# Unused products ahead of the second sums of squares and of the next layer's first chunk, at three layer crossings

## The reference, cut to what matters

```
y_l, y_c = mixer(h_l, h_c, need_ctx=need_ctx)          # ends with a product: (...) @ w_out
x_lat = x_lat + gt_l * rmsnorm(y_l, g_post)            # first root of a mean of squares
x_ctx = x_ctx + gt_c * rmsnorm(y_c, g_post)
# next layer
h_l = rmsnorm(x_lat, g_pre) * (1.0 + sc_l) + sh_l      # second root of a mean of squares
h_c = rmsnorm(x_ctx, g_pre) * (1.0 + sc_c) + sh_c
...  = h @ w_in
```

## Time and profile before

| | |
|---|---|
| median of 3 runs | 2997.91 us |
| profiled execution | 2989.49 us, span 2987.6 us |
| TensorE products (PE) busy | 2793.4 us, 93% of the span |
| TensorE weight loads (PEld) busy | 2298.3 us, 77% |
| VectorE (DVE) busy | 1565.3 us, 52% |
| ScalarE (ACT) busy | 1223.8 us, 41% |
| GpSimd (POOL) busy | 886.4 us, 30% |
| granted TensorE clock, mean | 0.977 |

### The profile page before, as it was taken

How to read it: one execution, slowest core, us unless ns; L and a number is a source line. 1 busy time by engine, 2 the same in 40 slices (tenths; PEclk the granted TensorE clock), 3 DMA queues, 4 the chain that set the end, 5 groups by cost and what they waited for, 6 DMA issues and landing times.

```text
span 2987.6 us, 39329 instructions
## 1 busy us (share of the span) xinstructions
PE 2793.4 (93%) x15720; PEld 2298.3 (77%) x15720; DVE 1565.3 (52%) x3126; ACT 1223.8 (41%) x2112; POOL 886.4 (30%) x636
## 2 busy tenths in 40 slices
PE   6989989999999999999999979999899999989997
PEld 4766878777877788878977768777798878878785
DVE  6677290162842876760268471254537238562583
ACT  4335234553213222242268354544443236443582
POOL 4611564403553444433200123200323320124301
PEclk8999999999999999999999989999999999999998
DMA  8303452301333555541300121100211230123101
GB/s 319 134 29 120 183 211 85 113 1 71 114 113 116 216 191 190 217 155 57 106 16 2 57 86 70 57 1 21 107 57 66 97 141 13 66 85 131 46 2 71
DMA packets 54293, 293.73 MB, mean 98 GB/s; under 512 B 4512, under 2 KB 8928, under 8 KB 24288
## 3 DMA queue, kind: packets, MB, share of 16 engines
q1 hardware_dynamic: 22464, 163.59, 15.5%
q10 hardware_dynamic: 31648, 127.63, 11.3%
HBM read 268.10 MB, written 17.86 MB: 96 GB/s over the span
## 4 chain that ended last, share of the span: by engine, by line
PE 56%; DVE 11%; ACT 3%; issue 2%; PEldq 0%; DMA 0%; DVEq 0%; PEld 0%; ACTq 0%
PE psum L467 14%; PE psum L469 14%; PE psum L468 14%; PE psum L1919 2%; PE psum L3551 2%; PE psum L1759 2%; PE psum L1782 2%; PE psum L1940 2%; DVE pair_row L1973 1%; PE psum L1929 1%; DVE y L2617 1%; PE psum L1763 1%; PE psum L1771 1%; DVE pair_prob L1982 1%; ACT L1004 1%
## 5 line engine op out<-in xcount | busy, mean ns | idle before, releaser
L454 POOL TENSOR_TENSOR w_lo<-raw,w_hi 128x512 fp32r<-128x512 f32 x612 | 859.9, 1437 | 2042.8 <-ACT w_hi L462 2042.8
L467 PE MATMUL psum<-a_hi,w_hi 128*128 128x512 f32 (+1 forms) x1848 | 697.5, 377 | 48.5 <-DVE a_lo L1162 17.0
L468 PE MATMUL psum<-a_lo,w_hi 128*128 128x512 f32 (+1 forms) x1848 | 686.4, 371 | 0.0
L469 PE MATMUL psum<-a_hi,w_lo 128*128 128x512 f32 (+1 forms) x1848 | 685.9, 371 | 0.0
L467 PEld LDWEIGHTS psum<-a_hi,w_hi 128*128 128x128 f32 x1848 | 350.9, 190 | 120.8 <-issue 23.5
L468 PEld LDWEIGHTS psum<-a_lo,w_hi 128*128 128x128 f32 x1848 | 350.8, 190 | 63.5 <-issue 3.4
L469 PEld LDWEIGHTS psum<-a_hi,w_lo 128*128 128x128 f32 x1848 | 350.2, 189 | 61.5
L462 ACT ACTIVATE w_hi<-raw 128x2048 fp32r<-128x2048 f32 x153 | 292.5, 1912 | 241.0 <-DMA raw<-stream 209.0
L467 PE MATMUL psum<-w_hi,a_hi 128*128 128x256 f32 (+1 forms) x608 | 199.0, 327 | 5.2 <-DVE a_lo L2654 4.4
L905 DVE SCALAR_TENSOR_TENSOR ada_temp<-ada_ring,psum 128x1024 f32<-128x1024 f32 x160 | 185.7, 1217 | 28.4 <-ACT psum L1134 14.1
L468 PE MATMUL psum<-w_lo,a_hi 128*128 128x256 f32 (+1 forms) x608 | 194.1, 319 | 0.0
(11 more groups left out here) (431 smaller groups left out, 4723.1 us busy)
## 6 DMA issues: line engine op xcount, KB each, us to landing
raw<-stream SPq DMA_DIRECT2D x153, 1024.0 KB, 4.9
ada_ring<-ada ACTq DMA_DIRECT2D x72, 1024.0 KB, 6.2
x_in<-xres ACTq DMA_DIRECT2D x3, 3072.0 KB, 12.5
xres<-x_in ACTq DMA_DIRECT2D x3, 2048.0 KB, 8.4
partner<-gq ACTq DMA_DIRECT2D x4, 1024.0 KB, 9.5
xres<-x_in ACTq DMA_DIRECT2D x1, 3072.0 KB, 9.5
own_raw<-stream SPq DMA_DIRECT2D x3, 1024.0 KB, 5.1
xres<-x_in ACTq DMA_DIRECT2D x3, 1024.0 KB, 4.8
```

The costliest lines, as they stand in the source:

```text
L454: last = pool.tensor_tensor(k.lo_of(s)[:, cols], k.raw_of(s)[:, cols], k.hi_of(s)[:, cols].bitcast(F32), ALU.subtract)
L467: pe.matmul(out, lhs[0], rhs[0], start=start, stop=False)
L468: pe.matmul(out, lhs[0], rhs[1], start=False, stop=False)
L469: return pe.matmul(out, lhs[1], rhs[0], start=False, stop=stop)
```

## The change

Two kinds of edit. In `sum_up`, for the second sum only, TensorE now waits for four chunks' squares and then issues 24 unused products, ahead of the wait for `gathered`; as `sum_up` is shared, this is issued six times (three latent, three context). And `dense` gets `fill=10` in Bin, Cv and A3q, ahead of the first two tiles.

```
@@ sum_up @@
         if turn == 0:
             pe.wait_ge(*self.total_in)
         else:
+            pe.wait_ge(self.squared.sem, self.squared.at(4))
+            self.k.keep_busy(pe, self.k.psum[:, 7, :], 24)
             pe.wait_ge(self.gathered.sem, self.gathered.at(KC - 1))
         pe.matmul(self.k.psum[:, 7, 0:self.t1 - self.t0], self.k.cst("ones"), self.total[:, self.t0:self.t1],
                   start=True, stop=True).then_inc(self.summed.sem, 1)
@@ gqa_layer, section A3q @@
-          act_tile=into(q, ACT.Copy, parts, -A_SCALE), barrier=False, lead=2, fill=5 if both else 0,
+          act_tile=into(q, ACT.Copy, parts, -A_SCALE), barrier=False, lead=2, fill=5 if both else 10,
@@ mla_layer, section Bin @@
-    dense(k, block, ["Bin"], None, act_tile=take_raw, barrier=False, lead=2, n_banks=7, side=context,
+    dense(k, block, ["Bin"], None, act_tile=take_raw, barrier=False, lead=2, n_banks=7, fill=10, side=context,
@@ mlstm_layer, section Cv @@
-    dense(k, block, ["Cv"], None, barrier=False, lead=2, n_banks=7, side=context, act_tile=take_value,
+    dense(k, block, ["Cv"], None, barrier=False, lead=2, n_banks=7, fill=10, side=context, act_tile=take_value,
```

## The result

| | before | after |
|---|---|---|
| median, 5 runs each | 2997.91 us (2995.33 to 3000.24) | 3012.37 us (3010.43 to 3014.53) |
| ratio, 95% interval | | 1.0048 (1.0033 to 1.0062) |
| profiled execution | 2989.49 us, span 2987.6 | 3010.43 us, span 3008.6 |
| granted clock, mean | 0.977 | 0.986 |

The change makes the kernel slower, by 14.5 us in this measurement and by 17.5 us in the means of a second one (e5_again). Predicted was 3021, with 3011 to 3031 as range. The median lies in the range, but only 1.4 us above its lower end; the differences, +14.5 and +17.5, lie under the +20 to +28 that had 76%, and the first of them in the +8 to +15 of rival 3. The two profiled executions lie 20.9 us apart.

The account below looks back on a forecast made before the run. TensorE, busy 93% of the span, was taken to bound the kernel. Delays at six places summed to +23.1 us, giving 3012.6 on the profiled 2989.49 and, with the runs' median 8.4 us above it, 3021; range 3011 to 3031.

Parts of the forecast that it names:

- rival 3: Cost partly absorbed, by a hidden last context crossing or shorter VectorE steps: +8 to +15 us, 3006 to 3013; chance 10%.
- What an unused product costs: Each product leaves two records of 0.215 us: 24 products cost 10.3 us of TensorE, 10 cost 4.3 us.
- rival 1: Products are cheap, 24 in 2.6 us, and mostly fit into idle time: -8.5 us, 2989; chance 4%.
- The new wait binds nowhere: At all second sums TensorE arrives after the fourth square is done, so the 24 products begin on arrival.
- D: Context tokens, layer 1 to 2: only 2.71 us idle before, root 7.0 us late, tile 8 follows: +7.0 us.
- A: Latent tokens, layer 0 to 1: root 3.6 us late, warm leading group 10.9 us instead of 13.4: +1.5 us.
- Place by place: Delays at the six latent and context crossings: 1.5, 1.2, 3.6, 7.0, 1.5 and 8.3, together +23.1 us.
- Nothing behind takes it back: Behind the last context sum, from 2695 to 2760, TensorE waits only for that sum, so the delay stays.
- C: Latent tokens, layer 1 to 2: sum 3.6 us later, clock gives back nothing beyond the sum: +3.6 us.
- E: Latent tokens, layer 2 to 3: same course as the latent crossing of layer 0 to 1, +1.5 us.
- the bounds on GpSimd: GpSimd's weight work stretches VectorE's steps; falling otherwise beside shifted steps, it may move each crossing 1 to 2 us either way.
- F: Context tokens, layer 2 to 3: products run to 2703.3 instead of a sum at 2695.01, all TensorE's time: +8.3 us.

Follow-up runs that it names:

- e5_again: The changed kernel once more, unaltered, beside many runs of the kernel before on the same chip: ratio 1.0060, mean difference +17.5 us.
- e11: The change with 12 unused products instead of 24 at all six places, fill of 10 kept: ratio 1.0015 to the kernel before, +3.8 us.
- e8: Kernel before plus only the blocks of 24 in the three context crossings, no latent blocks, no fill: ratio 1.0059, mean difference +17.2 us.
- e2: The change without fill=10, the six blocks of 24 left: ratio 1.0090 to the kernel before, mean difference +28.5 us.
- e1: The kernel before, unchanged, profiled a second time: ratio 0.9994, profiled execution 2991.98 us.
- e4: The change without the context blocks: 24 products ahead of the latent second sums, fill of 10 kept; ratio 1.0013 to the kernel before, +5.1 us.

## Why the prediction was right, and where its size was off

- **What an unused product costs** (10.3 us for 24): right. The blocks take 10.36 us from their start to the sum, e11 gives 0.43 us a product a second time. The short price, rival 1, is refuted. (Two small slips in the prediction change nothing: four times 109 ns for 24 products is 10.5 us, not 10.3, and the upper bound of the places is 25.2, not 25.3.)
- **The new wait binds nowhere**: right. No row of a block has a bracket in the profile after, so they begin where TensorE arrives (e8, sum 3 to 4: D grows by 7.5 us, which is 10.3 less an idle time of 2.7).
- **The clock.** That blocks and fill keep it up: right (1.00 throughout). That the gain is the warm leading group and the warm sum: right, e2 shows that the fill is needed for it. Its size in A goes by one profile: the leading group lasts 11.1 us instead of 13.4 there, and 12.6 in the second profile of the kernel before (e1), where the clock came up earlier.
- **Place by place**: right to 0.2 us between the two profiled executions, 23.0 against 23.1. Some of this closeness is luck: with e1 in place of the profile before, A is +2.2 and D +7.4, and the sum +24.0.
- **"Nothing behind takes it back"**: right. From the last marks of the third crossing to the end the distance between the two profiles only shrinks from 21.7 to 21.0, that of the spans.
- **The step whose size was off** is the one from the profile to the runs: "The median of the runs lies 8.4 us above this execution; the same 23.1 on it gives 3021". It takes whatever makes other executions longer as something that the change leaves alone. Behind it stands the reading "the sum begins there instead of 1738.82": I took the idle time of 5.47 us ahead of the latent sums, three times nearly equal, for a constant of the kernel. It has two values, 5.5 and 8.7, and in the profiled execution all three crossings had the small one. In a crossing that goes the long way the block of 24 covers 3.26 us more. For C this is measured once: 48.77 us from sum 1 to 3 with the block, 48.32 in e8's second crossing without, so +0.45 instead of +3.6. For A and E it is an estimate, 1.4 less 3.26 = -1.9, as no profile has these two the long way without products.
- How far this explains the runs: the places, +23.0 on the all-short 2989.49, give 3012.5 for the changed kernel, and its mean was 3012.2 both times. So the differences of 14.3 and 17.5 follow from how far the kernel before lay above 2989.49, 8.4 and 5.2 us. At 3.26 us a crossing these would be 2.6 and 1.6 crossings of three the long way; the eleven of 24 counted in the profiles would be 1.4. That the whole offset is this and nothing else isn't shown. All-short executions differ too (2989.49, 2991.98 in e1, and single runs of the kernel before go down to 2984.4), three crossings of 3.26 can make 9.8 us of a spread of 14, and by the same sum e4 should be 2995.8 (mean 2997.0) and e2 3016.4 (mean 3020.4). Why the share of the long way should differ from chip to chip stays open.
- The sentence in the bounds on GpSimd ("each crossing may move by 1 to 2 either way") had the cause in view and half its size, but as a shift that could go either way. The profile was all on the short side, so against it other executions of the kernel before can only be longer. Rival 3 named a smaller difference too, but not for this reason: F wasn't hidden (+8.35).

## What to carry to other kernels

On this kernel, unused products that keep the clock up are paid in full (0.43 us each) from the moment at which the wait that they fill would have ended: count them against the idle time of each place, and don't share one count between places with 8.4, 2.7 and 1.8 us. A helper that is called from several places (here both kinds of crossing) carries an edit to all of them. And an idle time read from one execution is one draw: profile the same kernel more than once and look at the spread of its runs before fitting anything to tenths of a microsecond. Two profiles wouldn't have been enough here: before and e1 are both the short way in all three crossings.

## What was not expected of the hardware

GpSimd and VectorE, both on 512-column f32 tensor operations with two inputs, slow each other when they overlap: VectorE's pair of 1.29 us takes 3.48, and GpSimd's first operation takes 3.47 where VectorE's pair goes ahead of it, 1.7 where it doesn't. With GpSimd's start 0.42 us ahead of VectorE's either can win, with nothing between (25.2 or 28.45 us for the stretch), and the outcome changes from one execution of the same program to the next, by a step of 3.26 us. Most other distances repeat to about 0.02 us; those in which the clock comes up don't (20.07 to 20.85 from sum 2 to 3 in the first crossing).

The Trainium skill, page "SBUF — State Buffer", section "SBUF: two separate sides", says that the two engines share a pair of ports that is locked as a whole, and that the one which starts first holds it for its whole instruction while the other blocks. The blocking agrees with these rows (1.29 against 3.48, 3.47 against 1.7). That the first to start wins doesn't show in the trace: GpSimd's record begins first in all 36 crossings, by 0.42 to 0.44 us, and in 19 of them VectorE's pair still goes through untouched. (A record's start need not be the moment at which the ports are taken, so the rule itself isn't refuted.) What decides between the two isn't shown by any run here.
